# Seven block products for 14 of 22 column groups of the gate and up matmuls, two weight sums on GpSimd

## The reference

```python
D_MODEL, SEQ, N_META, D_FF = 1024, 512, 16, 2816

def rms_norm(x, w):
    y = x * lax.rsqrt(jnp.mean(x * x, axis=-1, keepdims=True) + NORM_EPS)
    return y * w

def swiglu(x, w_gate, w_up, w_down):
    return (jax.nn.silu(x @ w_gate) * (x @ w_up)) @ w_down
```

## Time and profile before

| | |
|---|---|
| median of three runs | 2161.76 us (2159.58 to 2163.03) |
| the profiled execution | span 2156.5 us |
| PE busy | 2130.4 us, 99% of the span |
| DVE, ACT, POOL busy | 47%, 35%, 5% |
| granted TensorE clock | 1.00 in all 40 slices of the profile |
| gate and up phases, from the first matmul to the first of the next phase | 13 to 277, 735 (shared with the norm before it) to 1005, 1135 to 1394, 1780 to 2024 us |

### The profile page before, as it was taken

How to read it: one execution, slowest core, us unless ns; L and a number is a source line. 1 busy time by engine, 2 the same in 40 slices (tenths; PEclk the granted TensorE clock), 3 DMA queues, 4 the chain that set the end, 5 groups by cost and what they waited for, 6 DMA issues and landing times.

```text
span 2156.5 us, 38308 instructions
## 1 busy us (share of the span) xinstructions
PE 2130.4 (99%) x16006; PEld 2013.1 (93%) x16006; DVE 1009.6 (47%) x1390; ACT 763.9 (35%) x1259; POOL 100.0 (5%) x97
## 2 busy tenths in 40 slices
...
GB/s 130 92 96 88 95 116 82 84 80 50 50 31 2 79 88 88 88 97 114 94 57 89 88 88 97 106 96 63 86 79 69 50 69 97 89 97 88 99 106 78
DMA packets 328974, 179.69 MB, mean 83 GB/s; under 512 B 15849, under 2 KB 323344, under 8 KB 328878
## 3 DMA queue, kind: packets, MB, share of 16 engines
...
q0 software_dynamic: 1024, 2.86, 0.5%
...
## 4 chain that ended last, share of the span: by engine, by line
PE 96%; DVE 2%; ACT 1%; DMA 0%; issue 0%; POOL 0%; SPq 0%; DVEq 0%; ACTq 0%
PE psum L608 70%; PE psum L620 10%; PE psum L834 6%; PE psum L2434 1%; PE psum L2493 1%; DVE w_hl L523 1%; PE psum L2992 1%; PE psum L1895 0%; PE psum L3008 0%; PE psum L3003 0%; DMA stage<-ffn_w_gate 0%; PE psum L1907 0%; DVE rinv L1411 0%; PE psum L711 0%; PE psum L687 0%
## 5 line engine op out<-in xcount | busy, mean ns | idle before, releaser
L608 PE MATMUL psum<-x_hl,w_hl 128*128 128x264 f32 (+1 forms) x9120 | 1239.1, 297 | 3.9 <-DVE w_hl L523 3.5
L608 PEld LDWEIGHTS psum<-x_hl,w_hl 128*128 128x128 f32 x9120 | 1178.2, 188 | 58.2 <-issue 7.4
L523 DVE TENSOR_TENSOR w_hl<-stage,w_hl 128x1024 fp32r<-128x1024 f32 (+1 forms) x310 | 396.4, 1279 | 347.9 <-ACT w_hl L516 347.8
L516 ACT ACTIVATE w_hl<-stage 128x1024 fp32r<-128x1024 f32 (+1 forms) x310 | 339.7, 1096 | 222.3 <-PE psum L608 95.6
L608 PE MATMUL psum<-acts,w_hl 128*128 128x264 f32 x2376 | 288.9, 284 | 0.0
L608 PEld LDWEIGHTS psum<-acts,w_hl 128*128 128x128 f32 x2376 | 288.6, 188 | 0.0
L1453 DVE TENSOR_TENSOR t_both<-psum,rinv 128x528 f32<-128x528 f32 (+1 forms) x88 | 61.9, 703 | 304.3 <-PE psum L608 304.3
L1254 ACT ACTIVATE acts<-t_both 128x528 f32 (+3 forms) x88 | 56.6, 644 | 399.6 <-DVE t_both L1456 399.6
L620 PE MATMUL psum<-x_hl,w_hl 128*128 128x264 f32 (+1 forms) x1344 | 172.2, 287 | 0.7 <-DVE w_hl L523 0.5
L620 PEld LDWEIGHTS psum<-x_hl,w_hl 128*128 128x128 f32 x1344 | 166.0, 188 | 2.7 <-DVE w_hl L523 0.9
L1447 DVE TENSOR_TENSOR t_both<-psum,rinv 128x528 f32<-128x528 f32 (+1 forms) x88 | 61.9, 704 | 181.8 <-PE psum L608 181.7
...
## 6 DMA issues: line engine op xcount, KB each, us to landing
stage<-ffn_w_gate SPq DMA_DIRECT2D x88, 512.0 KB, 3.8
stage<-ffn_w_up SPq DMA_DIRECT2D x88, 512.0 KB, 3.8
...
stage<-odd_w_in SPq DMA_DIRECT2D x24, 512.0 KB, 3.9
stage<-ffn_w_down SPq DMA_DIRECT2D x22, 512.0 KB, 3.4
stage<-even_w_in SPq DMA_DIRECT2D x18, 512.0 KB, 3.9
stage<-even_w_out SPq DMA_DIRECT2D x8, 512.0 KB, 3.7
stage<-odd_w_out SPq DMA_DIRECT2D x8, 512.0 KB, 3.5
```

The costliest lines, as they stand in the source:

```text
L516: act.activation(weights(core.w_hl[:, slot.ring, 0, :], *kind), weights(core.stage[:, slot.stage, :], *kind), ACT.Copy).then_inc(core.w_hi, 1)
L523: dve.tensor_tensor(weights(core.w_hl[:, slot.ring, 1, :], *kind), weights(core.stage[:, slot.stage, :], *kind), weights(core.w_hl[:, slot ...
L608: op = pe.matmul(out, lhs, moving[:, moved, kt, t0:t0 + n], start=first and part + moved == 0, stop=last and part == 1)
```

## The change

In groups 4 to 17 of each gu phase (`SEVEN_FROM, SEVEN = 4, 14`) gate and up tile together are taken as a 2 x 2 block matrix (rows: lower and upper half of the 1024 features; columns: gate and up), the activations as a 2 x 2 block matrix too (token halves x feature halves), and their product is made with seven block products in place of eight. A block product is 4 feature tiles x 3 = 12 matmuls of 264 columns (256 in TAIL), so a group has 84 where it had 96 (48 of 512 in TAIL).

- Such a group has four slots: three with two block products and one with one. Their weights are (1) the gate tile, (2) two sums made by VectorE (`weight_sums`: "column", and "both" = column + gate's lower half), (3) two sums made by GpSimd in the load buffer, in place (`weight_sums_in_place`), (4) the upper half of the up tile. All four are split into high and low, 3584 elements per partition in place of 2048. Groups 4, 6, 8, ... load into a second pair of buffers (`spare`). GpSimd's first addition reads "both", and the low split of slot 2 overwrites it, so that split waits for it.
- The seven products add up in three PSUM banks. ScalarE copies partial results out between them (`seven_kept`, four copies of 264 columns), and TensorE waits for each copy (`product_kept`) before it adds further products to that bank. VectorE puts the results together (`seven_outputs`: three additions and two products of 264 columns), ScalarE applies silu.
- The sums of activations need the norm's factor inside: VectorE scales the 8 activation tiles (`scaled_tiles`, 8 operations of 528 elements in slots 1 and 2), makes four sums of quarters (`quarter_sums`, 1056 elements each, slots 3 and 4), and the four sums and the four plain quarters are split again: 8 copies by ScalarE (`x_high`) and 8 low parts by VectorE (`x_low`), two in each of slots 4 to 7. The plain quarters are written over the old `x_hl`, so `plain_by_halves` runs group 3 one token half after the other, and the first half's quarters are overwritten after its products.
- From group 4 on results need no scaling. The products of groups 4 to 17 stay as f32 in `acts_raw`; their high and low parts are made in groups 18 to 21 (`kept_tiles`, up to three per slot).
- In groups 2 and 3 TensorE waits for the scaling of both slots of the group before. Before, a slot waited for the one four slots earlier.
- The loops of the gu phases are written out, and some semaphores are merged to free their numbers.

The diff, cut to its core:

```diff
 HALF = TOK // 2
+SEVEN_FROM, SEVEN = 4, 14
+KEPT_FROM = SEVEN_FROM
...
+def group_stage(core, n, side, slot):
+    if is_seven(n) and (n - SEVEN_FROM) % 2 == 0:
+        return core.spare[:, side, :]
...
+def load_groups(core, sp, a, phase):
...
+        for side, slot in enumerate(group_slots(phase, n)[0:2]):
...
+            if is_seven(n):
+                stage_landed(core, sp, phase, n - 1, side)
+            if n == SEVEN_FROM:
+                sp.wait_ge(core.slot_used, phase.slot0 + 1)
+            elif n:
+                sp.wait_ge(core.w_lo, stage_left(phase, n, side))
...
+            w = (a["ffn_w_up"] if side else a["ffn_w_gate"])[phase.layer, phase.ffn]
+            src = w[:, n * P:(n + 1) * P].rearrange("(k p) n -> p k n", p=P)
+            sp.dma_start(weights(group_stage(core, n, side, slot), DT, P), src)\
...
+def plain_by_halves(core, pe, phase, n):
+    k = core
+    slots = group_slots(phase, n)
+    for part in range(2):
+        for slot in slots:
+            if part == 0:
+                pe.wait_ge(k.w_lo, slot.count())
+                pe.wait_ge(k.scaled, phase.evac0 + 2 * (n - 1))
+            bank = 2 * slot.pair + (0 if phase.cols == TAIL else part)
+            for kt in range(DT):
+                op = part_products(k, pe, phase, slot, kt, kt, k.x_hl, part, bank, kt == 0, kt == DT - 1)
+            if part:
+                op.then_inc(k.slot_used, 1)
+            elif slot is slots[-1]:
+                op.then_inc(k.product_made, 1)
+S_M5, S_M6, S_M7, S_M3 = range(4)
+A11, A12, A22, A21 = range(4)
+A_PLACES = ((0, 0), (DT // 2, 0), (DT // 2, 1), (0, 1))
...
+def seven_products(core, pe, phase, n):
+    k = core
+    j = phase.seven0 + n - SEVEN_FROM
+    sum_bank, first_bank, second_bank = seven_banks(phase, n)
+    slots = group_slots(phase, n)
...
+    def product(slot, unit, bank, moving, start):
+        w = parts(phase.cols)[0][1]
+        for kt in range(DT // 2):
+            for side, moved in ((0, 0), (0, 1), (1, 0)):
+                at = (unit * (DT // 2) + kt) * P
+                op = pe.matmul(k.psum[:, bank, 0:w], k.w_hl[:, slot.ring, side, at:at + P], moving(moved, kt),
+                               start=start and kt + side + moved == 0, stop=kt == DT // 2 - 1 and side == 1,
+                               skip_group_check=not start)
+        return op
...
+    pe.wait_ge(k.w_lo, slots[0].count())
+    pe.wait_ge(k.act_full, phase.a0 + n - 1)
+    pe.wait_ge(k.x_lo, phase.x0 + 4 + A11 + 1)
+    product(slots[0], 0, sum_bank, plain(A11), True).then_inc(k.product_made, 1)
+    pe.wait_ge(k.x_lo, phase.x0 + 4 + A12 + 1)
+    product(slots[0], 1, first_bank, plain(A12), True).then_inc(k.slot_used, 1)
+    pe.wait_ge(k.w_lo, slots[1].count())
+    pe.wait_ge(k.product_kept, 4 * j + 1)
+    product(slots[1], 0, sum_bank, summed(S_M6), False).then_inc(k.product_made, 1)
+    product(slots[1], 1, second_bank, summed(S_M7), True).then_inc(k.slot_used, 1)
+    pe.wait_ge(k.w_lo, slots[2].count())
+    pe.wait_ge(k.product_kept, 4 * j + 2)
+    product(slots[2], 0, sum_bank, summed(S_M5), False).then_inc(k.product_made, 1)
+    pe.wait_ge(k.x_lo, phase.x0 + 4 + A22 + 1)
+    pe.wait_ge(k.product_kept, 4 * j + 3)
+    product(slots[2], 1, second_bank, plain(A22), False).then_inc(k.slot_used, 1)
+    pe.wait_ge(k.w_lo, slots[3].count())
+    pe.wait_ge(k.product_kept, 4 * j + 4)
+    product(slots[3], 0, sum_bank, summed(S_M3), False).then_inc(k.slot_used, 1)
...
+def seven_split_hi(core, act, phase, n, r):
+    k = core
+    slot, second = group_slots(phase, n)[r], group_slots(phase, n)[1]
+    j = phase.seven0 + n - SEVEN_FROM
+    width = DT * P
+    if r == 0:
+        act.wait_ge(k.w_landed[slot.stage], slot.landed())
+        src = group_stage(k, n, 0, slot)
+    elif r == 1:
+        act.wait_ge(k.weights_sum, 4 * j + 2)
+        src = k.ring_raw[slot.ring][:, 0:width]
+    elif r == 2:
+        act.wait_ge(k.weights_sum, 4 * j + 4)
+        src = group_stage(k, n, 0, slot)
+    else:
+        act.wait_ge(k.weights_sum, 4 * j + 1)
+        width = width // 2
+        src = group_stage(k, n, 1, second)[:, width:2 * width]
+    act.wait_ge(k.slot_used, slot.count(RING))
...
+        act.wait_ge(k.x_summed, q0 + DT)
+        if part:
+            act.wait_ge(k.slot_used, group_slots(phase, SEVEN_FROM - 1)[1].count())
+        else:
+            act.wait_ge(k.product_made, products_before(phase, SEVEN_FROM))
+        src, dst = k.scaled_x[:, kt0:kt0 + DT // 2, cols], k.x_hl[:, 0, kt0:kt0 + DT // 2, cols]
+    act.activation(dst, src, ACT.Copy, scale=-1.0 if q == S_M6 else 1.0).then_inc(k.x_hi, 1)
+X_HIGH_AT = {4: (0, 1), 5: (2, 3), 6: (4, 5), 7: (6, 7)}
...
+def seven_kept(core, act, phase, n, r):
...
+    if r == 0:
+        act.wait_ge(k.act_full, phase.a0 + n - 1)
+        act.wait_ge(k.product_made, products_before(phase, n) + 1)
+        keep(gate, first, sum_bank)
+    elif r == 1:
+        if n == SEVEN_FROM:
+            act.wait_ge(k.scaled, phase.evac0 + 2 * n)
+        act.wait_ge(k.product_made, products_before(phase, n) + 2)
+        keep(gate, second, sum_bank)
+        act.wait_ge(k.slot_used, slots[1].count())
+        keep(up, second, second_bank)
+    elif r == 2:
+        act.wait_ge(k.product_made, products_before(phase, n) + 3)
+        keep(up, first, sum_bank)
+    else:
+        act.wait_ge(k.halves_made, 2 * j + 1)
+        cols = token_cols(gate[:, :], phase.cols)
+        act.activation(cols, cols, ACT.Silu).then_inc(k.gate_silu, 1)
...
+def weight_sums(core, dve, phase, n):
...
+    w11, w12, w22 = gate[:, 0:w], up[:, 0:w], up[:, w:2 * w]
+    both, column = raw[:, 0:w], raw[:, w:2 * w]
+    dve.wait_ge(k.w_landed[slots[1].stage], slots[1].landed())
+    dve.wait_ge(k.slot_used, slots[1].count(RING))
+    dve.wait_ge(k.w_lo, slots[0].count())
+    dve.tensor_tensor(column, w12, w22, ALU.add).then_inc(k.weights_sum, 1)
+    dve.wait_ge(k.weights_sum, 4 * j + 1)
+    dve.tensor_tensor(both, column, w11, ALU.add).then_inc(k.weights_sum, 1)
...
+def weight_sums_in_place(core, pool, phase, n):
...
+    w11, w21, w12 = gate[:, 0:w], gate[:, w:2 * w], up[:, 0:w]
+    pool.wait_ge(k.weights_sum, 4 * j + 2)
+    pool.wait_ge(k.w_lo, slots[0].count())
+    pool.tensor_tensor(w21, both, w21, ALU.add).then_inc(k.weights_sum, 1)
+    pool.tensor_tensor(w11, w12, w11, ALU.add).then_inc(k.weights_sum, 1)
...
+def scaled_tiles(core, dve, phase, tiles):
+    k = core
+    t0 = parts(phase.cols)[0][0]
+    for kt in tiles:
+        col = phase.before.pre_col + kt
+        dve.scalar_tensor_tensor(k.scaled_x[:, kt, t0:TOK], k.h[:, kt, t0:TOK], k.norm_cols[:, col:col + 1],
+                                 k.rinv[:, t0:TOK], ALU.mult, ALU.mult).then_inc(k.x_summed, 1)
...
+def quarter_sums(core, dve, phase, which):
...
+    if which == S_M5:
+        dve.wait_ge(k.x_summed, q0 + DT)
+        op = dve.tensor_tensor(out, x22, x21, ALU.subtract)
+    elif which == S_M6:
+        dve.wait_ge(k.x_summed, q0 + DT + S_M5 + 1)
+        op = dve.tensor_tensor(out, k.seven_raw[:, S_M5, :, 0:w], x11, ALU.add)
+    elif which == S_M7:
+        op = dve.tensor_tensor(out, x11, x21, ALU.subtract)
+    else:
+        dve.wait_ge(k.x_summed, q0 + DT + S_M6 + 1)
+        op = dve.tensor_tensor(out, k.seven_raw[:, S_M6, :, 0:w], x12, ALU.subtract)
+    op.then_inc(k.x_summed, 1)
...
+def x_low(core, dve, phase, q):
+    k = core
+    half = parts(phase.cols)
+    w = half[0][1]
+    dve.wait_ge(k.x_hi, phase.x0 + q + 1)
...
+        op = dve.scalar_tensor_tensor(out, src, -1.0, hi.bitcast(F32), ALU.mult, ALU.subtract)
+    else:
+        op = dve.tensor_tensor(out, src, hi.bitcast(F32), ALU.subtract)
+    op.then_inc(k.x_lo, 1)
+TILES_AT = {1: range(0, DT // 2), 2: range(DT // 2, DT)}
+SUMS_AT = {3: (S_M5, S_M6), 4: (S_M7, S_M3)}
+X_LOW_AT = {4: (0, 1), 5: (2, 3), 6: (4, 5), 7: (6, 7)}
...
+def seven_outputs(core, dve, phase, n, r):
...
+    s = slots[r].local
+    if r == 0:
+        groups_ahead_lo(k, dve, phase, s)
+        dve.wait_ge(k.product_kept, 4 * j + 1)
+        dve.wait_ge(k.slot_used, slots[0].count())
+        dve.tensor_tensor(gate[:, one], gate[:, one], k.psum[:, first_bank, 0:w], ALU.add)
+    elif r == 1:
+        groups_ahead_lo(k, dve, phase, s)
+    elif r == 2:
+        if is_seven(n + 1):
+            weight_sums(k, dve, phase, n + 1)
+        dve.wait_ge(k.slot_used, slots[2].count())
+        dve.wait_ge(k.product_kept, 4 * j + 4)
+        dve.tensor_tensor(gate[:, two], gate[:, two], k.psum[:, second_bank, 0:w], ALU.add).then_inc(k.halves_made, 1)
+        dve.tensor_tensor(up[:, two], up[:, one], up[:, two], ALU.add).then_inc(k.halves_made, 1)
+        groups_ahead_lo(k, dve, phase, s)
+    else:
+        groups_ahead_lo(k, dve, phase, s)
+        dve.wait_ge(k.slot_used, slots[3].count())
+        dve.wait_ge(k.gate_silu, phase.a0 + n + 1)
+        dve.scalar_tensor_tensor(k.acts_raw[:, n, one], k.psum[:, sum_bank, 0:w], -1.0, gate[:, one], ALU.mult,
```

(7 more changed lines are left out.)

433 lines of the change are left out of this document (346 added, 87 removed).

## The result

The changed kernel takes 2167.59 us (median of nine runs, 2164.02 to 2169.0), the kernel before 2160.65 us beside it (nine runs, 2158.39 to 2163.03). The ratio is 1.0029, with a 95% interval of 1.0021 to 1.0038: slower by 0.3%. The forecast was 2170.0 us. The profiled execution spans 2161.9 us, 5.4 more than that of the kernel before.

The account below looks back on a forecast made before the run. TensorE was taken to bound the kernel. About 19 us of waiting against 15 to 18 saved in each phase gave +9 us: a span of 2165, a median of 2170 us, with an 8-in-10 range of 2151 to 2190.

Parts of the forecast that it names:

- What bounds it: Whole kernel: TensorE is busy 99% of the span, so only removing matmul columns gains and any TensorE wait loses.
- The pace and the chain: Seven-product groups: matmuls at 123.0 ns, 10.33 us a group; chain of 3.17 us against 2.95, so 0.2 us waiting.
- rival (a): GpSimd and VectorE don't exclude each other, matmuls run at 120.9 ns (118.5 at 256 columns); 2157 us, chance 0.16.
- Rival (c): The chain in the groups is longer than forecast; each 0.1 us costs 5.5 us, 0.3 gives 2187 us; chance 0.13.
- The head: Phase start: VectorE's queue delays group 4 by 11.0 us of waits, 8.6 of them for input quarter A11's low part.
- the lock: Head of a phase: GpSimd's additions keep VectorE out of two-input SBUF operations, holding a low split up 2.6 us.
- The copy of product 1: Group 4: product 3 waits for ScalarE's copy of product 1, 3.1 us more.
- Rival (b): TensorE's clock falls in the long wait; first products' slowdown hidden, perhaps 2 to 3 us left per phase; 2180 us, chance 0.15.
- The forecast is wrong if matmuls behind the first wait take 0.24 us: Sign against the forecast: matmuls at 0.24 us each behind the wait ahead of group 4.
- Group 17 and the end: TensorE waits 1.9 us in group 17 for group 18's late-loaded gate tile; work kept for groups 18 to 21 costs nothing.
- The sum: Per-phase totals: +0.9 us in the first, +1.6 in the second and third, +4.5 in the last; together +9 us.
- Rival (d): Queue at the head shorter because TensorE's waits drain it, half of the 11 us gone; 2150 us, chance 0.09.

Follow-up runs that it names:

- e3: Changed kernel with the seven-product form only in groups 6 to 17 and the quarter sums spread over slots 3 to 11; 2150.46 us, 0.9953 of the kernel before.
- e4: Changed kernel with quarters A11 and A12 split ahead of slot 6's weight sums and splits on both engines; 2175.51 us, 1.007 of the kernel before.
- b3: Changed kernel with groups 6 to 17 in seven-product form, ScalarE copies first and head work reordered, GpSimd sums kept; 2113.72 us, 0.9779 of the kernel before.
- e5: e4 plus 82 matmuls per phase with unread results, filling the two long waits of group 4; 2171.22 us, 1.0038 of the kernel before.
- e1: Changed kernel with ScalarE's copies ahead of its high split in slot 3, in group 17 also slot 2; 2137.63 us, 0.9893 of the kernel before.

## Why the prediction came out right, step by step

**What bounds it.** Right, but for the clock. TensorE's waits and columns moved the time, and its granted clock in e3, e4 and b3; e5 adds matmuls to e4 and gets shorter.

**The pace and the chain: right as a sum by luck, both terms off.** The forecast had 10.33 us of matmuls and 0.2 of waiting in a group; the period came out at 10.53 to the hundredth. e1 takes the sum apart: 10.17 and 0.36, two errors of 0.16 us that cancel. The pace of 123.0 ns that I took from the rows of L620 in the earlier trace rows was too high; 121.1 at 264 columns and 9.94 / 84 = 118.3 ns at 256 is what rival (a) assumed. It was the likeness that failed, not the reading: the successor of L620 still runs at (9.01 - 0.28) / 71 = 123.0 ns in the changed kernel (L713, the row of 790.10), the seven products don't. Why those rows are slower is open. The chain was right in length. Its rows in a steady group of the changed kernel:

```profile
834.21 4.51 PE L1239 MATMUL psum<-seven_x,w_hl 128*128 128x264 f32 x36
...
837.36 0.69 DVE L1864 TENSOR_TENSOR ring_raw<-stage 128x512 f32<-128x512 f32 x1 [0.57 <-PE psum L1239]
838.09 0.69 DVE L1866 TENSOR_TENSOR ring_raw<-ring_raw,stage 128x512 f32<-128x512 f32 x1
838.82 1.06 ACT L1500 ACTIVATE w_hl<-ring_raw 128x1024 fp32r<-128x1024 f32 x1 [1.12 <-DVE ring_raw L1866]
839.78 0.37 ACT L1616 ACTIVATE rinv<-psum 128x264 f32<-128x264 f32 x1
840.30 0.96 PE L1239 MATMUL psum<-seven_x,w_hl 128*128 128x264 f32 x6
```

Product 4 ends in the stream two products behind 834.21, at 834.21 + 24 x 0.1211 = 837.12; "column", "both", the split of "both", the copy, and TensorE at 840.30: 3.18 us, forecast 3.17. What I had too long was what TensorE does meanwhile, two products in 2.91, not 2.95. And I had left out the restart: product 7 takes 1.52 to the next (819.23 to 820.75), after no wait 1.44 (813.04 to 814.48 in e1). So 0.27 of waiting and 0.08 of restart. Rival (c) was thus half true in its size (0.16 us more in a group than forecast, in 13 groups of four phases, 52 and not the 55 of its text), and its effect was met by the pace of rival (a).

**The head.** The mechanism was right, its size 0.8 us too large. Group 4 started 33.6 us behind slot 4, forecast 34.4; the wait for A11 was 8.0 of the 8.6 that I gave it, the two before it 0.5 and 1.0 against 0.9 and 1.5. The order of the queue has the waits where I put them. In VectorE's own rows the mis-sized terms are its small waits (five of 0.1 us, 0.5 for 0.9), the lock (2.4 for 2.6) and the wait for ScalarE (0.7 for 0.8). That the length of the queue decides is shown by e3, which moves it, and by e4, which turns it around.

**The copy of product 1.** Product 3 was forecast 40.4 us behind slot 4 and came after 39.54, 0.9 early with the head; between group 4's start and it lay 6.0 us, forecast 6.1. But TensorE waited there for 0.33 us, not for 3.1: it spent the rest on two products at half the clock.

**Rival (b), the clock.** I had given it 0.15, and its first half came true: behind the long wait the granted clock was 0.50. It cost nothing, since the products 1 and 2 that it slowed lie under the wait for the copy, as the rival's own text had it. Its second half (2 to 3 us left in each phase) is false for the change, 0.99 from product 3 on. It comes true in e3, e4 and two phases of b3, where a wait stands in the open with no later one behind it. "The forecast is wrong if matmuls behind the first wait take 0.24 us" was a poor sign: they took (5.62 - 0.28) / 23 = 0.23 us, as good as met, and the sum held. The rule of the Trainium skill that I named (TensorE: Matmul & The Clock Gate, Part 1: The HAM clock gate) describes this trace, where 8.00 us of waiting were followed by a granted clock of 0.50.

**Group 17 and the end.** 1.44 us of waiting and 0.08 of restart for the 1.9 forecast. The engine work kept for groups 18 to 21 cost nothing: 384 matmuls in 46.59 us are (46.59 - 0.28) / 383 = 120.9 ns.

**The sum.** The second phase lasts from 773.52, less the 0.62 us that its first wait is longer than in the earlier trace rows, to 1005.43: 232.5 us, against 232.1 before (773.14 to 1005.24). That is +0.4; forecast was +1.6. The last phase takes 228.0 against 224.1: +3.9 for +4.5. The differences are the head (-0.8) and group 17 (-0.4). Over the whole execution the spans show +5.4 for the +8.6 forecast, the medians +6.9 for about +8. Here too errors cancel: a phase saves 14 x (11.60 - 10.17) = 20.0 us of matmuls where I had 17.8, and its groups wait 13 x 0.36 = 4.7 us where I had 2.6.

Rival (d), a queue that drains much shorter, is out: 0.8 us of it went, where the rival needed half of 11. Not tried is whether groups 18 to 21 could take the new form too.
